# Expert stage of a two-layer decoder step: dummy products on TensorE in places where it waits, and the last pair's second gate-and-up half issued ahead of the preceding pair's down products

## The chip, the cores and the metric

The kernel runs on one core of one Trainium2 chip. The metric is the device time of one execution in microseconds (us). Several runs are taken and the median is quoted.

## What is computed

One inference step of a two-layer decoder, in float32, for 512 prompt tokens and 32 sample tokens together (544 tokens of 1024 numbers). Layer 0 mixes by gated linear attention and a state-space scan, layer 1 by pooling and block-sparse attention. After each mixer comes a mixture of experts, the only part that the change touches besides the end of the routing before it:

```python
for g in range(N_GROUPS):                                  # 4 groups of 8 experts
    gate_g = jnp.where((grp == g)[:, None], gates, 0.0)    # two experts of one group per token
    hg, hu = jnp.split(jnp.einsum('nd,edf->nef', xt, w_gate_up[g]), 2, axis=-1)
    out = out + jnp.einsum('nef,efd->nd', jax.nn.silu(hg) * hu * gate_g[..., None], w_down[g])
```

Each of the 32 experts of a layer has a gate-and-up matrix of 1024 x 512 and a down matrix of 256 x 1024.

## The kernel before, in words

Each layer runs mixer, `settle_stage`, `expert_stage`, `combine_stage`. Each stage is a `Scope` with a block, and at the end of a block all five engines meet: each drains its own work, and none starts the next stage before the last has arrived.

`settle_stage` (L1159) multiplies by the output weights, normalizes, and routes: DVE computes for every slot of the expert stage which token sits there. TensorE (PE) helps with small products: ten that give the tokens (L1342, sent to DVE by `toks`), ten that give each slot's share (L1347). Between them stand calls of `idle_products` (L156), which multiply a constant identity matrix by constant ones, 128x256 each, into a PSUM bank that nobody reads. GpSimd (POOL) then gathers the token rows of pairs 0 and 1 (L1154, called from `rows`). SyncE (SP) has by then sent for the weights of pairs 0, 1 and 2: the ring has three places.

`expert_stage` (L1551) treats the experts in pairs: two experts, 64 slots each, share the 128 partitions. There are 16 fixed pairs (`main` is 16, numbers 0 to 15) and, where an expert got more than 64 tokens, extra pairs (16 and on) whose weights POOL gathers by index. Of this input layer 0 uses none and layer 1 uses one. A pair's steps on PE are:

- `x_T(i)` (L1645): transposes the gathered rows by eight products. ACT and DVE copy the result out of PSUM (L1714).
- `gate_up(i, 0)` and `gate_up(i, 1)` (L1660): eight matmuls each, for the first and the second half of the 1024 inputs. A half waits for its own half of the weights.
- ACT then takes SiLU of the gate part (L1745), DVE multiplies by the up part (L1766) and raises `hr`.
- `h_T(i)` (L1671): two transposes, copied by ACT (L1735).
- `down(i)` (L1684): eight matmuls. ACT and DVE scale the result by the slot's share (`copy_y`, L1722 and L1723), and POOL scatters it (L1596).

A float32 matmul shows as two records in the profile, so eight matmuls are counted as x16.

PE's order in iteration i of `run` is gate_up(i, 0), h_T(i-1), x_T(i+1), down(i-1), gate_up(i, 1). ACT's order in iteration i is: copy h_T(i-1), copy x_T(i+1), copy_y(i-1), SiLU(i). DVE's is: copy x_T(i+1), copy_y(i-1), multiply(i). SP sends for pair i's weights in three pieces, first halves, second halves, down (L1129, L1135), each when pair i-3 no longer needs its place (`gh`, `gu`, `dn`). After iteration 16, which holds only h_T(15) and down(15), PE reads the number of extra tiles and runs the extra pair.

Of the kernel before, what the change touches and what calls it, by code (L numbers as in the profile page):

```python
# [155 lines left out]
def idle_products(nc, C, out, n):  # L156

    for _ in range(n):
        nc.tensor.matmul(out[:, 0:256], C("ident"), C("ones").unsqueeze(1).to_broadcast([128, 2, 128]), start=True, stop=True)
# [999 lines left out]
def settle_stage(nc, name, C, X, lng, lnb, ln_T, mixT, w_dram, l, w_router, b_router, lg, xT, rows, E, back):  # L1159


    with Scope(nc, name) as s:
# [17 lines left out]
        hi, base, asel, pos = (s.sb(x, [128, 10]) for x in ("hi", "base", "asel", "pos"))  # L1180
# [13 lines left out]
        pp = [s.ps(f"p{i}") for i in range(3)]  # L1194
# [46 lines left out]
        def _(pe):  # L1241
# [104 lines left out]
            for n in range(10):  # L1346
                last = nc.tensor.matmul(pr[:, 0:NPAIR], ohr[:, n, :], ci[:, n, 1, :], start=(n == 0), stop=(n == 9))  # L1347
            last.then_inc(toks, 1)

        @block.vector  # L1350
        def _(dve):
# [199 lines left out]
def expert_stage(nc, name, C, E, xT, xd, yd):  # L1551
# [3 lines left out]
    main = NE // 2  # L1555
    parts = ((main, main + 1), (main + 1, NPAIR))
    with Scope(nc, name) as s:
# [6 lines left out]
        pg = [s.ps(f"g{i}") for i in range(2)]  # L1564
# [9 lines left out]
        def tiles_of(eng):  # L1574
            return eng.value_load(E.extra[0:1, 0:1], min_val=0, max_val=NTILE - NE)
# [60 lines left out]
        @block.tensor  # L1636
        def _(pe):
            def x_T(i):
                pe.wait_ge(xl[i % 2], 16 * (i // 2 + 1))
                if i >= 1:  # L1640
                    pe.wait_ge(xta, i)
                    pe.wait_ge(xtd, i)
                xv = xg[i % 2][:, :].rearrange("r (p j) -> r j p", j=KD)
                for j in range(KD):
                    last = nc.tensor.transpose(px[j // 4][:, (j % 4) * 128:(j % 4) * 128 + 128], xv[:, j, :], C("ident"))  # L1645
                last.then_inc(xt, 1)

            def gate_up(i, h):
                if i < main:
                    pe.wait_ge(E.up_in[h][i % NR], 32 * (i // NR + 1))  # L1650
                elif h == 0:
                    pe.wait_ge(wx[i % NR], 64 * ((i - main) // NR + 1))
                if h == 0:
                    pe.wait_ge(xta, i + 1)
                    pe.wait_ge(xtd, i + 1)
                    if i >= 2:
                        pe.wait_ge(hr, i - 1)
                for j in range(4 * h, 4 * h + 4):
                    for a in range(2):
                        last = nc.tensor.matmul(pg[i % 2][64 * a:64 * a + 64, :], xgT[i % 2][:, j, 64 * a:64 * a + 64],  # L1660
                                                wg[2 * (i % NR) + a][:, j * 512:(j + 1) * 512],
                                                start=(j == 0), stop=(j == KD - 1))
                last.then_inc((gh, gu)[h], 1)

            def h_T(i):
                pe.wait_ge(hr, i + 1)
                if i >= 1:
                    pe.wait_ge(htc, i)
                hv = hh.rearrange("r (p j) -> r j p", j=2)
                for j in range(2):  # L1670
                    last = nc.tensor.transpose(ph[:, j * 128:(j + 1) * 128], hv[:, j, :], C("ident"))  # L1671
                last.then_inc(ht, 1)

            def down(i):
                if i < main:
                    pe.wait_ge(E.down_in[i % NR], 32 * (i // NR + 1))
                pe.wait_ge(htc, i + 1)
                if i >= 1:
                    pe.wait_ge(ya, i)
                    pe.wait_ge(ydv, i)  # L1680
                for n2 in range(2):
                    for j in range(2):
                        for a in range(2):
                            last = nc.tensor.matmul(py[n2][64 * a:64 * a + 64, :], hT[:, j, 64 * a:64 * a + 64],  # L1684
                                                    wd[2 * (i % NR) + a][:, j * D + n2 * 512:j * D + (n2 + 1) * 512],
                                                    start=(j == 0), stop=(j == 1))
                last.then_inc(dn, 1)

            def run(lo, hi):
                x_T(lo)  # L1690
                for i in range(lo, hi + 1):
                    if i < hi:
                        gate_up(i, 0)
                    if i > lo:
                        h_T(i - 1)
                    if i + 1 < hi:
                        x_T(i + 1)
                    if i > lo:
                        down(i - 1)
                    if i < hi:  # L1700
                        gate_up(i, 1)

            run(0, main)
            tiles = tiles_of(pe)
            for (lo, hi), least in zip(parts, (0, 2)):
                with pe.If(tiles > least):
                    run(lo, hi)
# [838 lines left out]
def build(nc, A, cols, ncols):  # L2546
# [8 lines left out]
    with Scope(nc, "top") as S:  # L2555
# [18 lines left out]
        for l in range(2):  # L2574
            if l == 1:
                reset_stage(nc)
                mixer_cd(nc, A, C, X, xT, pages, kpages, table)
            reset_stage(nc)
            with Scope(nc, f"m{l}") as M:
                E = Experts(nc, A, M, l)  # L2580
                settle_stage(nc, f"n{l}0", C, X, A["ln_g"][l, 0], A["ln_b"][l, 0], A["ln_T"][l], xT, A["cd_w_out" if l else "ab_w_out"],
                             l, A["w_router"], A["b_router"], lg, xT, xd, E, lambda t: rows_at(l, t))
                expert_stage(nc, f"e{l}", C, E, xT, xd, yd)
                combine_stage(nc, f"n{l}1", C, X, A["ln_g"][l, 1], A["ln_b"][l, 1], yd, E,
                              xT=None if l else xT, rows=None if l else xs, out=(A["y_p"], A["y_s"]) if l else None)
# [57 lines left out]
```

## Time and profile before

| | us |
|---|---|
| median of 3 runs | 1393.95 (1393.51 to 1405.43) |
| the profiled execution | 1396.67 |
| its span, first to last instruction | 1394.9 |
| PE busy | 1122.1 (80%) |
| ACT busy | 249.2 (18%) |
| DVE busy | 482.1 (35%) |
| expert stage of layer 0 in the trace | from about 382 to 632 |
| expert stage of layer 1 in the trace | from about 1075 to 1350 |

Times inside the trace are microseconds from the start of the span. "Granted clock" is the share of full speed that the throttle gave TensorE: 1.00 is 2.4 GHz, 0.50 is 1.2 GHz, and a figure between them is a stretch that holds both. The DMA share is the mean busy share of the core's 16 DMA engines. A timeline row gives the start, the length, the engine, the line, what is written and read, the count of records, and in brackets how long the engine had been idle and what ended that.

### The profile page before, as it was taken

The page shows a single profiled execution, that of the slowest core. Times are in us where ns is not written, and L with a number is a line of the kernel's source. Part 1 is how long each engine was busy: PE and PEld are TensorE (multiplying, and loading weights), DVE is VectorE, ACT ScalarE, POOL GpSimd, SP SyncE. Part 2 cuts the span into 40 slices and gives each one's busy share as a digit, 9 for nine tenths or more (in the row PEclk, how much of TensorE's full clock was granted, in tenths as well). Part 3 has the DMA queues.
Part 4 walks back from the last instruction along what each step waited for, and adds up shares of the span by engine and source line. Part 5 has one row for each costly group of instructions (what it writes and reads, how often), then busy time and mean ns, then how long its engine had stood idle before and what let it go on. Part 6 is the DMA issues. An engine that isn't in the chain of part 4 may idle for free. (4 is left out here: it accounts for less than half of the span.)

```text
span 1394.9 us, 15206 instructions
## 1 busy us (share of the span) xinstructions
PE 1122.1 (80%) x5745; PEld 568.8 (41%) x5745; DVE 482.1 (35%) x1308; ACT 249.2 (18%) x529; POOL 192.7 (14%) x184
## 2 busy tenths in 40 slices
PE   7999999499799777880499998985997998878540
PEld 5865666355633222220243344543555333222110
DVE  3515665366611111115221333541766111111017
ACT  0311333111111111112111212241111111111011
POOL 0000000000011111003243542220000111111112
PEclk9999999799899999895599998996998999999775
DMA  6510100293579999944676997664915899999723
GB/s 255 192 63 1 61 1 1 104 406 128 211 293 420 420 420 420 421 198 177 264 278 243 394 361 273 242 249 154 421 57 213 344 418 420 420 421 420 312 92 145
DMA packets 84851, 360.41 MB, mean 258 GB/s; under 512 B 13858, under 2 KB 18083, under 8 KB 54819
## 3 DMA queue, kind: packets, MB, share of 16 engines
q1 hardware_dynamic: 60802, 276.47, 49.7%
q0 software_dynamic: 19808, 74.48, 13.9%
q10 hardware_dynamic: 4160, 8.39, 1.6%
q8 instruction: 51, 0.84, 0.2%
q14 instruction: 30, 0.24, 0.1%
HBM read 344.90 MB, written 31.16 MB: 270 GB/s over the span
## 5 line engine op out<-in xcount | busy, mean ns | idle before, releaser
L1660 PE MATMUL e_psum_g<-m_wg,top_xT 128*64 128x512 f32 x1056 | 264.7, 652 | 71.9 <-DMA m_wg<-in_moe_w_gate_up 69.2
L1660 PEld LDWEIGHTS e_psum_g<-m_wg,top_xT 128*64 128x64 f32 x1056 | 80.9, 149 | 246.7 <-issue 159.7
L1684 PE MATMUL e_psum_y<-m_wd,top_xT 128*64 128x512 f32 x528 | 123.4, 610 | 5.4 <-DMA m_wd<-in_moe_w_down 3.4
L1253 PE MATMUL n_psum_p<-m_wg,top_xT 128*128 128x512 f32 x256 | 117.5, 606 | 0.0
L1714 DVE COPY top_xT<-e_psum_x 128x512 f32<-128x512 f32 x33 | 22.8, 692 | 214.2 <-PE e_psum_x L1645 214.2
L1154 POOL DMA_INDIRECT m_xg<-token_rows,m_tokof x33 | 33.5, 1016 | 456.6 <-PE e_psum_x L1645 241.7
L1951 PE MATMUL cd_psum_ab<-cd_w,top_xT 128*128 128x512 f32 x192 | 86.4, 603 | 0.0
L475 PE MATMUL ab_psum<-ab_w,top_xT 128*128 128x512 f32 x192 | 85.2, 597 | 0.0
L1800 POOL DMA_INDIRECT cd_kv<-in_cache_kT,top_kpages x64 | 62.0, 968 | 98.5 <-PE cd_psum_d L1993 44.3
L460 PE MATMUL ab_psum<-top_xT,ab_w 128*128 128x272 f32 x320 | 73.9, 393 | 1.0 <-DMA ab_w<-in_ab_w_in 1.0
L1723 DVE TENSOR_SCALAR e_Y<-e_psum_y,m_share 128x512 f32<-128x512 f32 x33 | 24.8, 751 | 129.0 <-PE e_psum_y L1684 129.0
L1253 PEld LDWEIGHTS n_psum_p<-m_wg,top_xT 128*128 128x128 f32 x256 | 47.4, 193 | 50.1 <-issue 49.9
L460 PEld LDWEIGHTS ab_psum<-top_xT,ab_w 128*128 128x128 f32 x320 | 60.6, 190 | 14.7 <-DMA ab_w<-in_ab_w_in 1.9
L1684 PEld LDWEIGHTS e_psum_y<-m_wd,top_xT 128*64 128x64 f32 x528 | 36.2, 139 | 67.7 <-issue 60.0
L1596 POOL DMA_INDIRECT expert_rows<-e_Y,m_dest x33 | 32.7, 992 | 201.0 <-DVE e_Y L1723 200.7
L1951 PEld LDWEIGHTS cd_psum_ab<-cd_w,top_xT 128*128 128x128 f32 x192 | 36.0, 193 | 48.4 <-issue 47.6
L475 PEld LDWEIGHTS ab_psum<-ab_w,top_xT 128*128 128x128 f32 x192 | 35.5, 190 | 43.4 <-issue 41.7
L1766 DVE TENSOR_TENSOR top_xT<-top_xT,e_psum_g 128x256 f32<-128x256 f32 x33 | 13.9, 421 | 108.7 <-ACT top_xT L1745 108.7
L1735 ACT ACTIVATE top_xT<-e_psum_h 128x256 f32<-128x256 f32 x33 | 12.7, 385 | 204.2 <-PE e_psum_h L1671 204.2
L1233 POOL MEMSET m_xg<- 128x1024 f32 x4 | 3.7, 949 | 303.9 <-POOLq L144 303.9
L220 PE MATMUL n_psum_t<-top_consts,top_X 128*128 128x128 f32 (+1 forms) x40 | 8.9, 401 | 43.1 <-DVE top_X L251 43.1
L1809 POOL DMA_INDIRECT cd_kv<-in_cache_v,top_pages x32 | 31.9, 998 | 82.7 <-PE cd_psum_e L2034 65.9
(432 smaller groups left out, 1438.1 us busy)
## 6 DMA issues: line engine op xcount, KB each, us to landing
m_wg<-in_moe_w_gate_up SPq DMA_DIRECT2D x128, 1024.0 KB, 25.9
m_wd<-in_moe_w_down SPq DMA_DIRECT2D x64, 1024.0 KB, 25.7
cd_kv<-in_cache_kT SPq DMA_DIRECT2D x64, 256.0 KB, 7.2
ab_w<-in_ab_w_in SPq DMA_DIRECT2D x4, 2048.0 KB, 7.6
m_wg<-expert_rows SPq DMA_DIRECT2D x16, 512.0 KB, 7.6
cd_w<-in_cd_w_in ACTq DMA_DIRECT2D x4, 2048.0 KB, 13.8
m_wg<-in_ab_w_out SPq DMA_DIRECT2D x2, 2048.0 KB, 10.6
token_rows<-top_X SPq DMA_DIRECT2D x8, 512.0 KB, 3.8
```

The costliest lines, as they stand in the source:

```text
L460: last = mm(out[:, 0:HALF], w[i][:, k, c0:c0 + 128], xT[:, k, HALF * h:HALF * h + HALF], start=(k == 0), stop=(k == KD - 1))
L475: last = mm(out[:, :], xT[:, k, tok0(t):tok0(t) + 128], w[i][:, k, :], start=(k == 0), stop=(k == KD - 1))
L1154: pool.indirect_dma_start(out=self.xg[i % 2][:, :], out_offset=None, in_=xd, in_offset=bass.IndirectOffsetOnAxis(ap=self.tokof[:, i:i + 1] ...
L1253: last = nc.tensor.matmul(pp[(2 * i + h) % 3][:P, :], mixT[:, k, tok0(t):tok0(t) + P], w[h][:, k, :], start=(k == 0), stop=(k == KD - 1))
L1596: nc.gpsimd.indirect_dma_start(out=yd, in_=Y[i % 2][:, :], in_offset=None, out_offset=bass.IndirectOffsetOnAxis(ap=E.dest[:, i:i + 1], axi ...
L1660: last = nc.tensor.matmul(pg[i % 2][64 * a:64 * a + 64, :], xgT[i % 2][:, j, 64 * a:64 * a + 64], wg[2 * (i % NR) + a][:, j * 512:(j + 1) ...
L1684: last = nc.tensor.matmul(py[n2][64 * a:64 * a + 64, :], hT[:, j, 64 * a:64 * a + 64], wd[2 * (i % NR) + a][:, j * D + n2 * 512:j * D + (n ...
L1714: ins = nc.scalar.activation(dst, src, ACT.Copy) if half == 0 else nc.vector.tensor_copy(dst, src)
L1723: nc.vector.tensor_scalar(dst, py[half][:, :], share, None, ALU.mult)
L1800: pool.indirect_dma_start(out=self.slots[slot][:, b, 512 * j:512 * j + 512], out_offset=None, in_=self.k_rows, in_offset=bass.IndirectOffs ...
L1809: pool.indirect_dma_start(out=self.slots[slot][:, b, :], out_offset=None, in_=self.v_rows, in_offset=bass.IndirectOffsetOnAxis(ap=self.pag ...
L1951: last = nc.tensor.matmul(out[:, :], xT[:, k, tok0(t):tok0(t) + 128], w[r][:, k, :], start=(k == 0), stop=(k == KD - 1))
```

## The change

It adds four groups of dummy products and moves one call. Two products stand at the end of PE's part of `settle_stage`, two at the start of PE's part of `expert_stage`, and four ahead of gate_up(i, 0) for each i from 4 to 14, behind a wait that gate_up(i, 0) has anyway. For i = 15, gate_up(15, 1) is issued right behind gate_up(15, 0), so ahead of h_T(14) and down(14). The extra pairs' `run(16, 17)` and `run(17, ...)` don't meet either condition. ACT, DVE, POOL and SP keep their code.

```diff
@@ settle_stage, tensor
             last.then_inc(toks, 1)
+            idle_products(nc, C, pp[1], 2)
@@ expert_stage, tensor
             def run(lo, hi):
                 x_T(lo)
                 for i in range(lo, hi + 1):
+                    if 4 <= i < main - 1:
+                        if i >= 2:
+                            pe.wait_ge(hr, i - 1)
+                        idle_products(nc, C, pg[i % 2], 4)
                     if i < hi:
                         gate_up(i, 0)
+                    if i == main - 1:
+                        gate_up(i, 1)
                     if i > lo:
                         h_T(i - 1)
                     if i + 1 < hi:
                         x_T(i + 1)
                     if i > lo:
                         down(i - 1)
-                    if i < hi:
+                    if i < hi and i != main - 1:
                         gate_up(i, 1)

+            idle_products(nc, C, pg[1], 2)
             run(0, main)
```

PE at the change of stage, before. `L159` is the dummy product, `L1347` the shares, the two branches are the end of one block and the start of the next, `L1645` is x_T(0) and `L1660` gate_up(0, 0).

```order
L159 MATMUL n_psum_p<-top_consts 128x256 x3
L1347 MATMUL n_psum_r<-top_xT 128x24 x10
L1162 UNCONDITIONAL_BRANCH
L1636 UNCONDITIONAL_BRANCH
L1645 MATMUL e_psum_x<-top_consts,m_xg 128x128 x8
L1660 MATMUL e_psum_g<-m_wg,top_xT 64x512 x8
```

The same place after the change (line numbers behind the first added line are one higher):

```order
L1347 MATMUL n_psum_r<-top_xT 128x24 x10
L159 MATMUL n_psum_p<-top_consts 128x256 x2
L1162 UNCONDITIONAL_BRANCH
L1637 UNCONDITIONAL_BRANCH
L159 MATMUL e_psum_g<-top_consts 128x256 x2
L1646 MATMUL e_psum_x<-top_consts,m_xg 128x128 x8
L1661 MATMUL e_psum_g<-m_wg,top_xT 64x512 x8
```

Two products now stand on each side of the branches, and those of the new stage stand ahead of x_T(0).

PE at the end of the fixed pairs, before. The first row holds gate_up(14, 1) and gate_up(15, 0); then come h_T(14), down(14), gate_up(15, 1), h_T(15), down(15).

```order
L1660 MATMUL e_psum_g<-m_wg,top_xT 64x512 x16
L1671 MATMUL e_psum_h<-top_consts,top_xT 128x128 x2
L1684 MATMUL e_psum_y<-m_wd,top_xT 64x512 x8
L1660 MATMUL e_psum_g<-m_wg,top_xT 64x512 x8
L1671 MATMUL e_psum_h<-top_consts,top_xT 128x128 x2
L1684 MATMUL e_psum_y<-m_wd,top_xT 64x512 x8
L1575 TENSOR_LOAD m_extra
```

The same place after:

```order
L1661 MATMUL e_psum_g<-m_wg,top_xT 64x512 x24
L1672 MATMUL e_psum_h<-top_consts,top_xT 128x128 x2
L1685 MATMUL e_psum_y<-m_wd,top_xT 64x512 x8
L1672 MATMUL e_psum_h<-top_consts,top_xT 128x128 x2
L1685 MATMUL e_psum_y<-m_wd,top_xT 64x512 x8
L1576 TENSOR_LOAD m_extra
```

gate_up(15, 1) has moved up, and nothing is left between down(14) and h_T(15).

ACT at the same place, in both kernels alike (here with the line numbers of before): copy of h_T(14), copy_y(14), SiLU(15), copy of h_T(15), copy_y(15).

```order
L1735 ACTIVATE top_xT<-e_psum_h 128x2x128
L1722 ACTIVATE e_Y<-e_psum_y,m_share 128x512
L1745 ACTIVATE top_xT<-e_psum_g 128x256
L1735 ACTIVATE top_xT<-e_psum_h 128x2x128
L1722 ACTIVATE e_Y<-e_psum_y,m_share 128x512
L1575 TENSOR_LOAD m_extra
```

## Rows read from the trace of the kernel before

**Rows 1.** Stretches: PE, PEld, DVE, ACT, POOL busy (x), clock, DMA share, GB/s.

```profile
420.00:440.00 20.00, 20.00 (x102) 7.99 (x100) 3.31 (x5) 3.72 (x7) 3.04 (x3) 1.00 1.02 421
...
580.00:600.00 20.00, 15.28 (x62) 5.27 (x60) 1.86 (x3) 2.05 (x4) 0.98 (x1) 0.83 1.01 419
```

**Rows 2.** Waits in layer 0's expert stage, 380 to 620: us, times, longest.

```profile
PE e_psum_g L1660 <- DMA m_wg<-in_moe_w_gate_up: 31.7, 9, 6.2
```

**Rows 3.** Timeline of PE, 403 to 451: a pair with its weights there.

```profile
403.21 7.04 PE L1660 MATMUL e_psum_g<-m_wg,top_xT 128*64 128x512 f32 x32
...
410.52 1.06 PE L1645 MATMUL e_psum_x<-top_consts,m_xg 128*128 128x128 f32 x8
...
414.99 7.04 PE L1660 MATMUL e_psum_g<-m_wg,top_xT 128*64 128x512 f32 x32
...
450.34 3.60 PE L1660 MATMUL e_psum_g<-m_wg,top_xT 128*64 128x512 f32 x16
```

**Rows 4.** Line 1162, end of layer 0's routing block: duration ns, start us.

```profile
L1162 POOLq DRAIN  x1: 4868/4868/4868, 377.2 to 377.2; - x1
L1162 PEldq DRAIN  x1: 2195/2195/2195, 377.8 to 377.8; - x1
```

**Rows 5.** Timeline around layer 0's first products; the last is layer 1's.

```profile
367.62 5.50 PE L159 MATMUL n_psum_p<-top_consts 128*128 128x256 f32 x16
...
382.33 1.94 PE L1645 MATMUL e_psum_x<-top_consts,m_xg 128*128 128x128 f32 x8 [2.35 <-PEq L1162]
...
385.14 5.21 PE L1660 MATMUL e_psum_g<-m_wg,top_xT 128*64 128x512 f32 x16 [0.87 <-DVE top_xT L1714]
...
1077.79 5.34 PE L1660 MATMUL e_psum_g<-m_wg,top_xT 128*64 128x512 f32 x16 [0.88 <-DVE top_xT L1714]
```

**Rows 6.** Stretches of one microsecond, columns as in rows 1.

```profile
371.00:372.00 1.00, 1.00 (x5) 0.83 (x5) 1.00 (x3) 0.00 (x0) 0.00 (x0) 0.88 1.14 352
...
381.00:382.00 1.00, 0.00 (x0) 0.00 (x0) 0.00 (x0) 0.00 (x0) 0.00 (x0) 0.74 0.29 103
...
615.00:616.00 1.00, 1.00 (x8) 0.40 (x6) 0.00 (x0) 0.00 (x0) 0.59 (x1) 1.00 0.02 8
```

**Rows 7.** Timeline, end of layer 0's fixed pairs.

```profile
601.96 7.22 PE L1660 MATMUL e_psum_g<-m_wg,top_xT 128*64 128x512 f32 x32
...
609.11 0.50 PE L1671 MATMUL e_psum_h<-top_consts,top_xT 128*128 128x128 f32 x2
...
610.13 3.65 PE L1684 MATMUL e_psum_y<-m_wd,top_xT 128*64 128x512 f32 x16 [0.52 <-issue]
613.59 3.63 PE L1660 MATMUL e_psum_g<-m_wg,top_xT 128*64 128x512 f32 x16
613.83 0.69 ACT L1722 ACTIVATE e_Y<-e_psum_y,m_share 128x512 f32<-128x512 f32 x1 [3.79 <-PE e_psum_y L1684]
...
617.26 0.38 ACT L1745 ACTIVATE top_xT<-e_psum_g 128x256 f32<-128x256 f32 x1 [2.75 <-PE e_psum_g L1660]
617.67 0.42 DVE L1766 TENSOR_TENSOR top_xT<-top_xT,e_psum_g 128x256 f32<-128x256 f32 x1 [3.10 <-ACT top_xT L1745]
618.15 0.50 PE L1671 MATMUL e_psum_h<-top_consts,top_xT 128*128 128x128 f32 x2 [0.93 <-DVE top_xT L1766]
...
619.17 3.65 PE L1684 MATMUL e_psum_y<-m_wd,top_xT 128*64 128x512 f32 x16 [0.52 <-issue]
```

**Rows 8.** Timeline, end of layer 1's fixed pairs.

```profile
1300.49 6.62 PE L1660 MATMUL e_psum_g<-m_wg,top_xT 128*64 128x512 f32 x16 [9.98 <-DMA m_wg<-in_moe_w_gate_up]
...
1312.77 3.65 PE L1660 MATMUL e_psum_g<-m_wg,top_xT 128*64 128x512 f32 x16 [1.04 <-DMA m_wg<-in_moe_w_gate_up]
...
1321.27 6.47 PE L1684 MATMUL e_psum_y<-m_wd,top_xT 128*64 128x512 f32 x16 [3.41 <-DMA m_wd<-in_moe_w_down]
1327.67 1.16 PE L1645 MATMUL e_psum_x<-top_consts,m_xg 128*128 128x128 f32 x8
```

**Rows 9.** Timeline, gate_up(14, 0) of layer 0.

```profile
590.68 6.54 PE L1660 MATMUL e_psum_g<-m_wg,top_xT 128*64 128x512 f32 x16 [4.72 <-DMA m_wg<-in_moe_w_gate_up]
```

## The prediction, as it was made before the change was run

> **What bounds the kernel now.** I read the stretches of 20 us first, to see where the expert stages are and what is full there. From 403 on in layer 0, until about 605, the DMA engines are full: two of these stretches show a DMA share of 1.02 and 1.01 at 419 to 421 GB/s, while TensorE is busy for 20.00 us in the first and only 15.28 in the second [rows 1]. The waits say the same: gate_up waited for weights 9 times in layer 0, 31.7 us in all [rows 2]. The timeline gives the two rates. With its weights there, PE needs 414.99 - 403.21 = 11.78 us for a pair [rows 3]. A pair's weights are 2 x (2 + 1) MB of 2^20 bytes, 6.29 MB, or 15.0 us at 420 GB/s, in three pieces of 5.0 us. So in the middle of an expert stage PE has over 3 us to spare in each pair, and nothing done there on PE alone moves the end. PE decides in two places: at the start, where SP may not send for pair 3 before gate_up(0, 0) has freed its place, so every microsecond there shifts the full DMA stretch; and at the end, behind the last weights. A gain or loss at these two places comes straight through to the span, since the stages meet at a barrier. That is why I price only those, twice, once for each layer.
>
> **Price of a dummy product.** Eight of them take 5.50 us from 367.62 on [rows 5], at half clock until 0.24 us into the stretch 371 to 372 (its clock is 0.88) [rows 6]. That is 3.62 us at half and 1.88 us at full clock: (1.81 + 1.88) / 8 = 0.46 us each at full clock, 0.92 at half.
>
> **Two products at the end of the routing.** They lie behind the share products, whose drain on PE ends at 377.8 + 2.2 = 380.0. POOL is the last at that barrier: its drain, behind the gathers, ends at 377.2 + 4.87 = 382.1 [rows 4]. Two products make PE ready at 380.9, or at 381.8 at half clock. Cost nothing, hidden by POOL's drain; without that cover it would be 0.9 to 1.8.
>
> **Two products at the start of the expert stage.** PE starts x_T(0) at 382.33, right behind the barrier [rows 5], so these are in the open: +0.92 at full clock, +1.84 at half. What they may buy is the clock. It fell at about 381.5 (0.74 in 381 to 382) [rows 6], after the share products and 1.5 us of nothing, and stayed at half over x_T(0) and most of gate_up(0, 0). At full clock x_T takes 1.06 and half a gate_up 3.60 [rows 3]; here they took 1.94 and 5.21, in layer 1 5.34 [rows 5]. So a held clock gives 0.88 + 1.61 = 2.5 us in layer 0 and, taking the same x_T, 2.6 in layer 1. Net of the 0.92: -1.6 and -1.7, together -3.3. The bounds are -2.6 and +1.84 per layer (the first if the products cost nothing, the second if they run at half clock and buy nothing). I take the held clock, since the added 0.9 us of dense products in front of the barrier and 0.9 behind leave a gap of only about 1.3 us.
>
> **Four products ahead of gate_up(i, 0), i from 4 to 14.** Eleven groups a layer of 1.85 us, on an engine that has more than 3 us to spare per pair once it is caught up. For i = 4 to 6 PE still runs without waiting and falls back by 5.5 us; at 11.78 against 15.0 us a pair it has gained 4 x 3.2 = 13 us on the transfers by pair 4, so they don't run dry. Their wait for `hr` is one that gate_up(i, 0) has anyway; behind it on PE stands only gate_up(i, 0). They may save the clock in some waits: gate_up(14, 0) of layer 0 took 6.54 after a wait of 4.72 [rows 9] where 3.60 is the full-clock time. But the next thing that counts, gate_up(15, 0), starts as its weights land, so the 2.9 us go into a longer wait. Price 0; bounds -1 and +1.8 (one group in the open in layer 1, delaying what follows).
>
> **gate_up(15, 1) ahead of h_T(14) and down(14).** In layer 0 the row that holds gate_up(14, 1) and gate_up(15, 0) took 7.22 where 7.04 is usual [rows 3, 7], so the first half of pair 15's weights landed at about 605.5, and the second a piece later, near 610.5; the DMA engines are empty by 615 to 616 [rows 6], which fits the third piece. Before, PE filled that time with down(14), 610.13 to 613.8, and ran gate_up(15, 1) from 613.59 to 617.2 without a wait. From its end to down(15) 1.97 us pass: SiLU, multiply, h_T, copy, down from 619.17 to 622.82 [rows 7].
> After, PE waits from 609.1 to 610.5, runs gate_up(15, 1) to 614.1, h_T(14) and its copy take 1.0 as before, and down(14) ends at 614.1 + 1.0 + 3.65 = 618.8. One would now expect SiLU(15) and the multiply to be long done beside down(14). They are not: ACT's order is unchanged and has copy_y(14) ahead of SiLU(15), and copy_y(14) waits for down(14). DVE too has its copy_y(14) ahead of the multiply. So from the end of down(14) the chain is copy_y 0.05 + 0.69, SiLU 0.05 + 0.38, multiply 0.03 + 0.42, h_T 0.5, copy and the way to down 0.5: 2.7 us. down(15) runs from 621.5 to 625.1: +2.3. Bounds: +0.9 if the second half lands before 609.1, +5.3 if only at 613.6.
> In layer 1 the wait is longer: gate_up(15, 0) ended at 1307.1 and the second half landed at 1312.77; down(15) then waited for its own weights until 1321.27 and ran at half clock, 6.47, to 1327.7 [rows 8]. After, PE has nothing to do from 1307.1 to 1312.77. A gap of 3.41 and one of 4.72 ended at half clock [rows 8, 9], so gate_up(15, 1) takes about 6.5 and ends at 1319.3; down(14) ends at 1319.3 + 1.0 + 3.65 = 1323.9, down(15) starts 2.7 later, when its weights have long landed, and ends at 1330.3: +2.6. At full clock all through it ends at 1327.4, -0.3; that is the bound below, +4 (down(14) at half clock too, in part) the one above.
> Together +4.9.
>
> **Sum.** -3.3 + 4.9 = +1.6 us on the profiled execution's 1396.67 (span 1394.9). That execution lies 2.7 above the median 1393.95, with which I go: 1395.6. About 1%, 14 us, is what a measurement of this kernel can tell from no change.
>
> **Rivals.**
> The clock at the start isn't held. For: two dense products are few, and the clock fell under the share products, which kept PE busy but narrowly. Against: the fall came 1.5 us behind the share products, and now 0.9 us of dense products stands in just that gap. Then the post-barrier products cost +1.84 a layer and buy nothing: 3.7 + 4.9 = +8.6, 1402.6. This is the case on the slow side: its place is the barrier between routing and experts, and it decides as soon as the level falls before 382.2.
> The clock is held over the products but not over x_T(0). x_T has only transposes, and before the change the clock stayed at half through all 1.94 us of it and rose only inside gate_up [rows 5]. Then x_T gives back the 0.9 that the products cost, gate_up(0, 0) gains nothing, and the sum is 0 + 4.9, 1398.9. The Trainium skill, TensorE: Matmul & The Clock Gate, part 4 on the PE-mode transpose, has such a rule: transposes don't count as work for the clock gate in the way that matmuls do. That the clock stayed low through x_T agrees with it but doesn't show it.
> The tail costs little. If pair 15's second half lands early in layer 0 (+0.9) and the clock holds in layer 1 (-0.3), the sum is -3.3 + 0.6 = -2.7, 1391.3. For it: DMA landing times shift from run to run. Against: the gap of 5.7 us in layer 1.
> The change does what it says in its last part: SiLU and multiply hidden beside down(14). That would give 1.0 to 1.7 back per layer, but ACT's written order excludes it.
>
> **How the numbers follow.** My forecast 0.45, the clock lost at once 0.2, lost over x_T 0.15, a cheap tail 0.2. All four lie within 9 us of before, inside 1%. The range takes the cheap tail less some scatter of the runs, 1389.5, and the clock lost, 1402.5. That leaves 0.03 for faster by over 1%, 0.93 within, 0.04 for slower by over 1%.
>
> **What would show it.** Right: x_T(0) starts about 0.9 later behind the barrier and takes 1.06, gate_up(0, 0) takes 3.6; the next weights are sent for about 1.6 earlier; the full DMA stretch is as long as before; down(14) stands between gate_up(15, 1) and SiLU(15), with SiLU starting behind copy_y(14); down(15) of layer 0 begins 2.7 behind down(14)'s end. Wrong: SiLU(15) running beside down(14); an expert stage shorter or longer by over 5 us; waits for weights before pair 6; DMA shares well under 1.0 between 410 and 600.

## The result, and the profile after

Over 20 runs of each kernel the median went from 1397.53 to 1404.22 us (1398.95 to 1412.71): ratio 1.0048, 95% interval 1.0032 to 1.0063, so 6.7 us slower (4.5 to 8.8). The change is below the 1% that I called the bound of a single measurement, but it is clear of the noise of 20 runs. The 20 runs also put the kernel before 3.6 us above the median of three runs from which the prediction started. The profiled execution took 1403.31 us.

First the page of the kernel after.

```profile
span 1401.5 us, 15590 instructions
...
PE 1162.4 (83%) x5937; PEld 603.0 (43%) x5937; DVE 481.9 (34%) x1308; ACT 248.7 (18%) x529; POOL 192.6 (14%) x184
```

PE is busy for 40 us more, by the 96 dummy products (192 records). The bulk of the expert stages is as it was; here are two stretches, columns as in [rows 1]:

```profile
425.00:445.00 20.00, 20.00 (x100) 8.57 (x98) 2.56 (x4) 3.03 (x6) 3.04 (x3) 1.00 1.02 422
585.00:605.00 20.00, 17.21 (x76) 6.85 (x74) 1.86 (x3) 2.05 (x4) 0.98 (x1) 0.91 1.01 420
```

and the waits for weights in layer 0, 380 to 625 (us in all, times, longest), as in [rows 2]:

```profile
PE e_psum_g L1661 <- DMA m_wg<-in_moe_w_gate_up: 17.8, 8, 3.9
```

DMA is full as before. The wait for weights has shrunk from 31.7 to 17.8 us [rows 2], since dummy products now fill a part of it (with these products alone it is 14.1 and 17.4 in two profiles). The stages are no shorter for that, as the experiments tell.

**The start.** Line 1162 of the kernel after, end of layer 0's routing block (duration ns, start us), as in [rows 4]:

```profile
L1162 POOLq DRAIN  x1: 4911/4911/4911, 379.4 to 379.4; - x1
L1162 PEldq DRAIN  x1: 2675/2675/2675, 380.5 to 380.5; - x1
```

and PE's timeline there, as in [rows 5]:

```profile
382.03 1.11 PE L159 MATMUL n_psum_p<-top_consts 128*128 128x256 f32 x4
384.58 2.04 PE L159 MATMUL e_psum_g<-top_consts 128*128 128x256 f32 x4 [1.43 <-PEq L1162]
386.41 1.92 PE L1646 MATMUL e_psum_x<-top_consts,m_xg 128*128 128x128 f32 x8
389.21 5.96 PE L1661 MATMUL e_psum_g<-m_wg,top_xT 128*64 128x512 f32 x16 [0.88 <-DVE top_xT L1722]
```

PE's drain ends at 383.2, POOL's at 384.3: the two products at the end of the routing are hidden, as forecast. The two behind the barrier take 2.04 us, half clock. x_T(0) and gate_up(0, 0) are at half clock as before, and gate_up(0, 0) even takes 5.96, where it took 5.21. The stretches show the level (columns as in [rows 6]):

```profile
383.00:384.00 1.00, 0.14 (x1) 0.00 (x0) 0.00 (x0) 0.00 (x0) 0.00 (x0) 0.82 0.41 148
384.00:385.00 1.00, 0.42 (x1) 0.46 (x2) 0.00 (x0) 0.00 (x0) 0.00 (x0) 0.50 0.00 0
...
393.00:394.00 1.00, 1.00 (x4) 0.27 (x2) 0.00 (x0) 0.00 (x0) 0.00 (x0) 0.56 0.00 0
```

It fell at about 383.6, in the gap of 1.4 us behind the new products, and came back only at about 393.9, ten microseconds later. Counted from the end of the share products the fall came after 1.5 us, and before the change it came after 1.5 us too (381.5 against 380.0) [rows 5, 6]: the two products in front of the barrier didn't put it off.

**The end of the fixed pairs.** PE, ACT and DVE in layer 0, answering to [rows 7]:

```profile
610.54 3.65 PE L1661 MATMUL e_psum_g<-m_wg,top_xT 128*64 128x512 f32 x16 [1.37 <-DMA m_wg<-in_moe_w_gate_up]
616.10 3.65 PE L1661 MATMUL e_psum_g<-m_wg,top_xT 128*64 128x512 f32 x16 [1.91 <-DMA m_wg<-in_moe_w_gate_up]
...
620.71 3.65 PE L1685 MATMUL e_psum_y<-m_wd,top_xT 128*64 128x512 f32 x16 [0.52 <-issue]
624.40 0.69 ACT L1730 ACTIVATE e_Y<-e_psum_y,m_share 128x512 f32<-128x512 f32 x1 [3.79 <-PE e_psum_y L1685]
...
624.99 0.38 ACT L1753 ACTIVATE top_xT<-e_psum_g 128x256 f32<-128x256 f32 x1
625.40 0.42 DVE L1774 TENSOR_TENSOR top_xT<-top_xT,e_psum_g 128x256 f32<-128x256 f32 x1 [0.24 <-ACT top_xT L1753]
625.87 0.51 PE L1672 MATMUL e_psum_h<-top_consts,top_xT 128*128 128x128 f32 x2 [1.51 <-DVE top_xT L1774]
...
626.90 3.65 PE L1685 MATMUL e_psum_y<-m_wd,top_xT 128*64 128x512 f32 x16 [0.52 <-issue]
```

gate_up(15, 1) was done at 619.7. Its SiLU started at 624.99, behind copy_y(14), which waited for down(14). PE stood still for 1.91 us ahead of gate_up(15, 1) and for 1.51 ahead of h_T(15). In layer 1 (answering to [rows 8]) the wait ahead of gate_up(15, 1) is longer, 7.01 us, and ends at half clock:

```profile
1305.21 5.35 PE L1661 MATMUL e_psum_g<-m_wg,top_xT 128*64 128x512 f32 x16 [3.91 <-DMA m_wg<-in_moe_w_gate_up]
1317.57 5.99 PE L1661 MATMUL e_psum_g<-m_wg,top_xT 128*64 128x512 f32 x16 [7.01 <-DMA m_wg<-in_moe_w_gate_up]
```

### The profile page after: what moved, and what is told of

Read it like the earlier page. It is cut to its first block and busy times, and to the rows that moved or that the text cites. A ratio compares the mean times of both kernels' runs of the same rounds, so it can differ in the third digit from the quotient of the medians.

```text
span 1401.5 us, 15590 instructions
## 1 busy us (share of the span) xinstructions
PE 1162.4 (83%) x5937; PEld 603.0 (43%) x5937; DVE 481.9 (34%) x1308; ACT 248.7 (18%) x529; POOL 192.6 (14%) x184
## 5 line engine op out<-in xcount | busy, mean ns | idle before, releaser
L1661 PE MATMUL e_psum_g<-m_wg,top_xT 128*64 128x512 f32 x1056 | 261.1, 643 | 41.2 <-DMA m_wg<-in_moe_w_gate_up 38.4
L460 PEld LDWEIGHTS ab_psum<-top_xT,ab_w 128*128 128x128 f32 x320 | 62.4, 196 | 15.4 <-DMA ab_w<-in_ab_w_in 1.9
L159 PE MATMUL e_psum_g<-top_consts 128*128 128x256 f32 x184 | 48.0, 404 | 2.6 <-PEq L1162 2.6
L159 PEld LDWEIGHTS e_psum_g<-top_consts 128*128 128x128 f32 x184 | 34.0, 195 | 24.9 <-issue 21.2
## 6 DMA issues: line engine op xcount, KB each, us to landing
m_wg<-in_ab_w_out SPq DMA_DIRECT2D x2, 2048.0 KB, 10.5
```

What stands on the lines that cost most here:

```text
L460: last = mm(out[:, 0:HALF], w[i][:, k, c0:c0 + 128], xT[:, k, HALF * h:HALF * h + HALF], start=(k == 0), stop=(k == KD - 1))
```

## The experiments

Four measures come from each profile: from the end of the share products to x_T(1) ("start", one for each layer), from the end of down(14) to the beginning of down(15) ("gap"; left blank where gate_up(15, 1) still stands between the two), the length of the two expert stages together (end of the share products to the first load of the combine stage), and the ratio of times. What lies outside these stages scatters: in code that no kernel here changes, the share products of layer 0 ended anywhere from 379.4 to 387.3 us. The stages themselves scatter from profile to profile of one kernel, by up to 2.2 us for both together and by up to 7.0 us in one layer (246.9 and 253.9 with four products before the barrier), so I lean on start and gap, and for whole costs on the times.

| kernel | start, layers 0 and 1 | gap, layers 0 and 1 | both stages | ratio (95%) |
|---|---|---|---|---|
| before | 10.3, 10.2 | | 530.1 | |
| before, again | 10.5, 9.9 | | 531.1 | |
| after | 12.9, 12.7 | 2.5, 2.5 | 534.6 | 1.0048 (1.0032 to 1.0063) |
| after, again | 13.0, 9.9 | 2.5, 2.5 | 536.0 | |
| start products only | 10.2, 10.4 | | 531.8 | 1.0022 (0.9998 to 1.0046) |
| two before, four behind the barrier | 12.3, 11.0 | | 529.6 | |
| waits only | 10.4, 10.1 | | 529.4 | 1.0022 (1.0000 to 1.0044) |
| waits only, again | 10.3, 10.1 | | 529.3 | 1.0010 (0.9994 to 1.0027) |
| moved half only | 10.1, 10.3 | 2.5, 2.5 | 533.7 | 1.0036 (1.0015 to 1.0057) |
| moved half, early SiLU | 10.3, 10.1 | 1.1, 1.1 | 528.8 | 1.0012 (0.9987 to 1.0036) |
| whole change, early SiLU | 10.2, 9.9 | 1.1, 1.1 | 524.9 | 1.0022 (1.0003 to 1.0041) |
| four before the barrier | 7.9, 10.1 | | 525.8 | 0.9971 (0.9941 to 1.0001) |
| four before the barrier, again | 10.3, 7.7 | | 528.0 | 0.9948 (0.9932 to 0.9964) |
| four before, moved half, early SiLU | 8.1, 7.7 | 1.1, 1.1 | 527.2 | 0.9942 (0.9921 to 0.9963) |

### The parts alone

The start products alone (against the kernel before):

```diff
@@ settle_stage, tensor, at the end
+            idle_products(nc, C, pp[1], 2)
@@ expert_stage, tensor, ahead of run(0, main)
+            idle_products(nc, C, pg[1], 2)
```

> Only the two products at the end of the routing and the two at the start of the expert stage. Theory A (the loss is made at the start: the products behind the barrier run at half clock, in the open, and buy nothing): from the end of the share products to the start of x_T(1) 12.8 us in each layer where the kernel before has 10.2, so +2.6 twice; +5 us in all, 0.35%. Theory B (the scatter of the runs, and the start costs only what the two products do at full clock): at most +1 per layer, +2 us. Theory C (the loss is made by the products in the waits and by the moved half): no more than +1 us here.

The starts took 10.2 and 10.4 us, not the 12.8 of theory A. PE's timeline of layer 0 in this run:

```profile
387.65 2.04 PE L159 MATMUL e_psum_g<-top_consts 128*128 128x256 f32 x4 [1.39 <-PEq L1162]
389.49 1.51 PE L1646 MATMUL e_psum_x<-top_consts,m_xg 128*128 128x128 f32 x8
391.88 3.65 PE L1661 MATMUL e_psum_g<-m_wg,top_xT 128*64 128x512 f32 x16 [0.88 <-DVE top_xT L1716]
```

The two products run at half clock again, 2.04 us, but now the level rises inside x_T(0), and gate_up(0, 0) gets the full clock: the start takes 10.2 us, as without them. In layer 1 the level had already fallen inside the share products (2.86 us instead of 2.41) and came back within x_T(0). So the products behind the barrier pay 1.8 us and get it back, or don't, by when the level returns. The time, 3.1 us more (-0.3 to +6.5), leaves both open.

The products in the waits alone:

```diff
@@ expert_stage, tensor, run
+                    if 4 <= i < main - 1:
+                        if i >= 2:
+                            pe.wait_ge(hr, i - 1)
+                        idle_products(nc, C, pg[i % 2], 4)
```

> Only the four products ahead of gate_up(i, 0) for i from 4 to 14. Theory A: no change, within 1 us; the weights land no later, the time from x_T(1) to the end of the fixed pairs is as before in layer 0 (232.5 us from the start of x_T(1) to the end of down(15)) within 1 us. Theory C: PE, put back by 1.9 us a pair, holds the weights of later pairs back or stands in front of ones that have landed: +2 to +6 us.

> The products in the waits alone, once more. Its expert stages took 529.4 us together as the kernel before does (530.1, 531.1), but its time was 1.0022 (1.0000 to 1.0044). Theory A: no cost, the interval of this run holds 1 and the stages take 528 to 532 again. Theory C: 1.002 again and a place where the time is lost, outside the expert stages, since these are as long as before.

The stages took 529.4 and 529.3 us, the kernel before 530.1 and 531.1: no cost to be seen in them. The stretch of layer 0 for which 232.5 us were expected took 232.4 and 234.5, and 234.8 in the second profile of the kernel before. The times say +3.1 us (0.0 to 6.2) and +1.4 us (-0.8 to +3.8): one interval touches zero and the other holds it. Whether some 2 us are real stays open; no place for them was found.

The moved half alone:

```diff
@@ expert_stage, tensor, run
+                    if i == main - 1:
+                        gate_up(i, 1)
                     if i > lo:
                         h_T(i - 1)
...
-                    if i < hi:
+                    if i < hi and i != main - 1:
                         gate_up(i, 1)
```

> Only gate_up(15, 1) moved ahead of h_T(14) and down(14). Theory A: SiLU(15) starts behind copy_y(14), down(15) starts 2.5 to 2.8 us behind the end of down(14); down(15) of layer 0 ends about 2.9 us later after x_T(1) than before; layer 1 between -1 and +3; in all +2 to +5 us. Rival D (the end of the stage is set by the landing of the last scatter and gives the loss back): down(15) later by 2 to 3 us in layer 0, but the combine stage's first load later by under 1 us; in all within 1.5 us.

The gap is 2.54 and 2.53 us, and the time is 5.0 us longer (2.1 to 8.0): the only part whose interval is clear of zero. Rival D isn't borne out by this run: layer 0's combine stage loads its first rows 9.2 us behind the last down, about as long as before (9.4). In the other profiles this stretch of layer 0 takes 7.5 to 9.8 us, with the half moved or not, and 8.2 in layer 1 always.

Where the 5.0 us lie, the trace tells only in part. Layer 0 of this run:

```profile
609.30 9.82 PE L1660 MATMUL e_psum_g<-m_wg,top_xT 128*64 128x512 f32 x32 [3.98 <-DMA m_wg<-in_moe_w_gate_up]
...
626.27 3.65 PE L1684 MATMUL e_psum_y<-m_wd,top_xT 128*64 128x512 f32 x16 [0.52 <-issue]
```

Here gate_up(15, 0) ran mostly at half clock, and the second half of the weights had landed when it was done. From its start to the end of down(15) pass 20.6 us; the second profile of the kernel before, with gate_up(15, 0) at half clock too, has 20.3. In layer 1 the same stretch takes 28.6 us, inside the 26.0 to 30.9 of the eight profiles that leave the half where it was. Nor do the parts add up: the start products, the products in the waits and the moved half come to 3.1 + 3.1 + 5.0 = 11.2 us by their times (9.5 with the second measurement of the waits), the whole change to 6.7. Each part has an interval of 2.3 to 3.4 us on either side, so their sizes are known no better than that.

### Why the moved half costs

The same with SiLU and the multiply of pair 15 ahead of copy_y(14):

```diff
@@ expert_stage, scalar, run
-                    if i > lo:
+                    if i > lo and i != main - 1:
                         copy_y(i - 1, 0, act, ya)
                     if i < hi:
...
                         nc.scalar.activation(sg, pg[i % 2][:, 0:DE], ACT.Silu).then_inc(sl, 1)
+                    if i == main - 1:
+                        copy_y(i - 1, 0, act, ya)
@@ expert_stage, vector, run: the same for copy_y(i - 1, 1, dve, ydv) and the multiply
```

> The moved half, and for pair 15 SiLU on ACT and the multiply on DVE ahead of their copy_y(14). Theory A: down(15) starts about 1.2 us behind the end of down(14) instead of 2.6, so 1.4 us less per layer than with the moved half alone, and in layer 0 still about 1 us later than before, since PE waits for the second half's weights with down(14) undone. If ACT's order is not what delays down(15), the gap stays at 2.6.

Layer 0's timeline of that kernel, ACT, PE and DVE together:

```profile
613.18 3.65 PE L1660 MATMUL e_psum_g<-m_wg,top_xT 128*64 128x512 f32 x16 [2.35 <-DMA m_wg<-in_moe_w_gate_up]
...
617.59 0.38 ACT L1747 ACTIVATE top_xT<-e_psum_g 128x256 f32<-128x256 f32 x1
617.79 3.65 PE L1684 MATMUL e_psum_y<-m_wd,top_xT 128*64 128x512 f32 x16 [0.52 <-issue]
...
621.48 0.69 ACT L1724 ACTIVATE e_Y<-e_psum_y,m_share 128x512 f32<-128x512 f32 x1 [3.52 <-PE e_psum_y L1684]
...
622.07 0.38 ACT L1737 ACTIVATE top_xT<-e_psum_h 128x256 f32<-128x256 f32 x1
622.54 3.65 PE L1684 MATMUL e_psum_y<-m_wd,top_xT 128*64 128x512 f32 x16 [0.67 <-ACT top_xT L1737]
```

SiLU now stands at 617.59, ahead of down(14), and the gap falls from 2.54 to 1.10 us in both layers. That is the 1.4 us expected, twice, so the order on ACT and DVE is what delays down(15). The time goes from +5.0 to +1.7 us (-1.8 to +5.0), the same way, but the two intervals overlap. The wait of 2.35 us for the second half, with down(14) undone, stays: from the end of gate_up(15, 0) to the end of down(15) layer 0 takes 15.4 us, where it takes 13.6 in all eight profiles that leave the half where it was.

The whole change with the same repair:

> The whole change, with SiLU(15) and the multiply ahead of copy_y(14). Theory A: of the 4.5 to 6 us that the change costs the two expert stages, ACT's order makes 2.8, so 531.5 to 533 us are left, the rest from the start of the stages; down(15) 1.1 us behind the end of down(14); time 2 to 4 us above the kernel before. If ACT's order is a side matter, 535 as before.

The gaps are 1.11 and 1.14, the time +3.1 us (0.4 to 5.7) where the change as it stands has +6.7 (4.5 to 8.8). The stages took 524.9 us, under every theory; its profiled execution, 1391.6 us, was the fastest of its 12 runs, so I don't read that number as a price.

### The start: what lies in front of the barrier and what behind

Two products in front and four behind:

> Two products at the end of the routing and four, not two, at the start of the expert stage. If they run at half clock in the open, x_T(0) starts 3.7 us behind the barrier instead of 2.0; the clock is back before x_T(0) ends, gate_up(0, 0) takes 3.6, and x_T(1) starts 11 to 11.9 us behind the share products. If a held clock were to be had, x_T(0) would start 1.9 behind the barrier and x_T(1) at 9.7.

In layer 0 the four took 3.75 us, half clock, and the start 12.3 us. In layer 1 the level was still full when the first of them began, and it fell 0.3 us later, inside them (a timeline row, then two stretches with the columns of [rows 6]):

```profile
1077.35 3.47 PE L159 MATMUL e_psum_g<-top_consts 128*128 128x256 f32 x8 [1.03 <-PEq L1162]
```

```profile
1077.00:1078.00 1.00, 0.65 (x2) 0.62 (x3) 0.00 (x0) 0.00 (x0) 0.00 (x0) 0.82 0.00 0
1078.00:1079.00 1.00, 1.00 (x4) 0.75 (x3) 0.00 (x0) 0.00 (x0) 0.00 (x0) 0.50 0.00 0
```

They took 3.47 us and the start 11.0. So even a start of the products at full clock doesn't mean that the clock is held. In this run the two more products behind the barrier cost more than they gave back.

Four in front and none behind:

```diff
@@ settle_stage, tensor, at the end
+            idle_products(nc, C, pp[1], 4)
```

> Only four products at the end of the routing, none behind the barrier: they fill PE's wait for POOL's drain. Theory E (what counts is the gap that is left before the barrier): they end about 0.3 us before POOL's drain or up to 0.3 behind it, the clock holds, x_T(0) takes 1.06 and gate_up(0, 0) 3.6, and from the end of the share products to the start of x_T(1) pass 7.8 us instead of 10.2 in each layer: -2.4 twice. Theory F (the narrow share products count too little, whatever follows them): the clock falls inside these four products as it fell behind the share products, they run partly at half clock and end up to 1.5 us behind POOL's drain, and the start takes 10 to 11.5 us. In neither case over 5 us in all.

> The four products ahead of the barrier alone, once more, for its time against the kernel before (0.9971, 0.9941 to 1.0001 the first time) and for the two states of its start: 7.8 to 8.0 us from the share products to x_T(1) where the clock holds, about 10 where it falls during the share products. If the first time was luck of the scatter, 10 in both layers and no gain.

PE in layer 0 and then in layer 1 of the first of these runs:

```profile
382.65 2.41 PE L1347 MATMUL n_psum_r<-top_xT 128*128 128x24 f32 x20 [0.92 <-DVE top_xT L1520]
384.91 1.97 PE L159 MATMUL n_psum_p<-top_consts 128*128 128x256 f32 x8
387.37 1.13 PE L1646 MATMUL e_psum_x<-top_consts,m_xg 128*128 128x128 f32 x8 [0.49 <-PEq L1162]
389.38 3.65 PE L1661 MATMUL e_psum_g<-m_wg,top_xT 128*64 128x512 f32 x16 [0.88 <-DVE top_xT L1715]
...
1064.36 3.05 PE L1347 MATMUL n_psum_r<-top_xT 128*128 128x24 f32 x20 [0.88 <-DVE top_xT L1520]
1067.24 3.76 PE L159 MATMUL n_psum_p<-top_consts 128*128 128x256 f32 x8
1071.30 1.78 PE L1646 MATMUL e_psum_x<-top_consts,m_xg 128*128 128x128 f32 x8 [0.30 <-PEq L1162]
```

Each theory came true in one layer. In layer 0 the share products take 2.41, the four products 1.97, the gap to x_T(0) is 0.49, and the clock holds: 7.9 us. The four end 1.8 us behind the share products, so PE works through the place at which the level fell with two products there, 1.4 to 1.8 us behind. In layer 1 the clock fell inside the share products (3.05 instead of 2.41), the four ran at half clock past POOL's drain, and the start took 10.1, no worse than before. Of the six starts with four products in front, four held (7.7 to 8.1 us) and two fell in this way (10.1 and 10.3).

The last run adds the moved half with its early SiLU:

> Four products ahead of the barrier, none behind it and none in the waits, the moved half, and SiLU(15) and the multiply ahead of copy_y(14). Theory A: the moved half with the right order on ACT and DVE is worth about nothing (down(15) 1.1 us behind down(14), PE idle for 1.5 to 2.4 us ahead of gate_up(15, 1)), so the two expert stages together take 525 to 530 us, as with the four products alone, and the time is 0 to 4 us under the kernel before. If hiding SiLU beside down(14) is worth its 1.4 us a layer, 523 us or less.

0.9942 with the moved half, 0.9948 without: it is worth nothing that can be told. The version to keep is the four products in front of the barrier alone. It is 0.3% faster than the kernel before in one measurement, whose interval just touches no change, and 0.5% in the other, whose interval is clear of it. Not all of that is explained: four of six starts at -2.4 us are 3.2 us for the two layers, while the two measurements say 4.1 (-0.1 to 8.2) and 7.3 (5.0 to 9.5). Where the rest comes from stays open.

The kernel before and the changed kernel were each profiled a second time:

> The kernel before, unchanged, for the scatter of the expert stages from run to run. From the end of the share products to the combine stage's first load: 252.3 and 277.8 us in the profile known so far. If these stages are steady, within 1.5 us each; then the differences of 3 to 4 us of the other runs are real. If they scatter by 3 us, no single profile tells the parts apart.

> The changed kernel again. From the end of the share products to x_T(1): 12.9 and 12.7 us in its first profile, 10.2 and 10.4 with the same products in the run that had only those. If the moment at which the clock comes back varies from run to run, anything from 10 to 13 here; if the rest of the change delays it, 12.7 to 12.9 again. The two stages together 534.6 us, within 2.

The stages of the kernel before took 531.1 us, 1.0 from the first profile, but one by one they moved by 2.8 and 1.8. The changed kernel's starts took 13.0 and 9.9 us. So the long start, 12.7 to 13.0, comes in some executions and not in others.

## Why the prediction was wrong

**The bound** was read rightly: DMA full in the middle at 420 to 422 GB/s, and the loss made at the start and behind the last weights.

**Products in the waits**, priced at 0: right in the stages, with 1 to 3 us in the times that no place was found for.

**The moved half**, priced at +4.9: right in mechanism, and its time alone, +5.0 (2.1 to 8.0), is near. The chain of 2.7 us (its terms add up to 2.6) measured 2.54. In layer 0 the piece took 5.6 us to land and not 5.0, so the wait was 1.91 and not 1.4, and from the end of gate_up(15, 0) to the end of down(15) the changed kernel takes 16.4 us against 13.6, +2.7 where I had +2.3. In layer 1 gate_up(15, 1) took 5.99 at half clock, where I took 6.5; but the +2.6 there isn't shown. From the start of gate_up(15, 0) to the end of down(15) the three profiles with the half moved and the order as written take 28.4 to 29.2 us, inside the 26.0 to 30.9 of the eight others, where down(15) waits for its own weights.

**Products at the end of the routing**, priced at nothing: right, since POOL's drain still ended last. They bought nothing either: with two of them there the level fell 1.4 to 1.8 us behind the end of the share products in eight of ten starts (the other two: 2.3 us behind, and inside the share products), and without any it fell 1.1 to 1.8 us behind in ten of twelve (the other two: inside).

**Products at the start of the expert stage**: here the prediction failed, at the step "I take the held clock". It stood for -3.3 us. In all eight starts with this pair of products (four profiles of three kernels, two layers each) the level was at half when they ran, and x_T(0) began 3.9 to 4.2 us behind the share products instead of 1.2 to 2.5. Three of the eight lasted 12.7 to 13.0 us and five 9.9 to 10.4, mean 11.1; twelve starts without them lasted 9.9 to 10.5, mean 10.2. So the term is +0.9 us a layer, +1.8 in all, and in the first profile of the changed kernel +5.2. The reason I gave, that 0.9 us of dense products on each side would bridge the gap, was wrong on its first half: behind the two products the clock fell in the gap of 1.1 to 1.5 us in seven of the eight starts, and in the eighth already in the share products. That the fall before the change stood 1.5 us behind the share products was my argument against it, and the fall came at that same place. With 1.97 us of them and gaps of 0.3 to 0.7 us it held in four of six. The rival "the clock at the start isn't held" is what happened. It had priced +1.84 a layer and 1402.6, and left out that the level may also come back earlier or later. With the pair of products it came back 5.0 to 5.8 us behind the share products in five starts, where gate_up(0, 0) took 3.65, and about 11.7 us behind in three, where it took 5.96 to 6.10; without them it was 7.9 to 9.2 us. What decides between 5 and 11.7 stays open: both came in one execution of one kernel. (That rival's 1402.6, to which I gave 0.2, also lies just outside the range that I stated.)

**The rival of the transposes** isn't supported as I used it: with the clock held over the four products in front of the barrier it also stayed at full over x_T(0) and the 0.88 us behind it, in all four such starts. By the rule that the prediction took from the Trainium skill (TensorE: Matmul & The Clock Gate, part 4), that transposes don't count as busy in the same way, the level could be at risk there; no start here showed a fall over x_T alone.

**The sum.** With the start at +1.8 in place of -3.3 the terms give 4.9 + 1.8 = +6.7 us, which is the measured difference. That is in part luck: the +1.8 is a mean of starts that lie 3 us apart, the first profile of the changed kernel alone has +5.2, and the +4.9 is borne out by a time with 3 us on either side while its half for layer 1 isn't shown in a trace. The point of departure, the median of three runs, was 3.6 us low, and that put 1404.22 outside a range that ended at 1402.5.

## What to carry to other kernels

Moving one engine's work earlier gives nothing if the engines that use its result keep their written order: read the followers' order first, here copy_y ahead of SiLU. And it gives nothing, even with the order mended, if the moved work then waits for its data with other work undone behind it, here 1.9 to 2.4 us in layer 0. Dummy work to hold TensorE's clock belonged, in this kernel, in the wait that another engine set, up to its very end, and not behind the barrier, where it was paid at half clock in the open. And filling waits with it where transfers set the pace changed the wait's name in the profile and gained no time.

## What the runs showed of the hardware

The granted clock fell in a gap of only 1.43 us behind 1.11 us of dense products and narrow products before them. In five of the 28 starts it fell inside the narrow share products themselves (128x24 each, 0.9 us of idle before them, 2.41 us at full clock, 2.84 to 3.08 where it fell in them), and in one start inside dense products, 0.3 us after they had begun behind a gap of 1.03 us. So an engine that reads as busy can lose its clock. After the fall it stayed at half for about 10 us in three of the four starts of the changed kernel (383.6 to 393.9 in layer 0 of the first profile), with PE busy in all but the gap and 0.9 us behind x_T(0), and came back after 3.4 us in the fourth.

POOL took long to drain at this barrier: 4.4 to 5.0 us from the beginning of the drain to its end, with two gathers of 128 rows just ahead of it. That is the wait in which TensorE's dummy products were free.
